# U's high part times both parts of x2 in one 480-column product, with an identity product to add the second half

## The reference, cut to what matters

```python
h = jnp.einsum('chkd,cd->chk', u, xt)          # rows of expert_u times x2
a = gt * jax.nn.gelu(h, approximate=False)
return jnp.einsum('chk,chkd->cd', a, vv)       # rows of expert_v
```

## Time and profile before

| | |
|---|---|
| median of 3 runs | 2293.77 us |
| the profiled execution | 2294.18 us, its span 2292.4 us |
| TensorE matmul busy, granted clock | 2269.2 us (99%), 0.998 |
| VectorE / ScalarE / POOL busy | 1716.0 / 1115.2 / 627.4 us |
| the chain that ended last, by line | line 812 30%, line 494 19%, line 847 17%, line 497 12%, line 853 9% |

### The profile page before, as it was taken

How to read it: one execution, slowest core, us unless ns; L and a number is a source line. 1 busy time by engine, 2 the same in 40 slices (tenths; PEclk the granted TensorE clock), 3 DMA queues, 4 the chain that set the end, 5 groups by cost and what they waited for, 6 DMA issues and landing times.

```text
span 2292.4 us, 45385 instructions
## 1 busy us (share of the span) xinstructions
PE 2269.2 (99%) x15683; PEld 2109.4 (92%) x15683; DVE 1716.0 (75%) x2311; ACT 1115.2 (49%) x1477; POOL 627.4 (27%) x442
## 2 busy tenths in 40 slices
PE   9999999999999999999999999999999999999997
PEld 8888899888898899999999999999999998998996
DVE  5544566655744577999999999998788887776767
ACT  4444555553343344555555455554554445444444
POOL 1000100000001026878756656557100000004000
PEclk9999999999999999999999999999999999999999
DMA  9888644566454656888878888888998997778874
GB/s 368 268 269 270 196 148 148 163 212 220 156 184 132 193 170 138 188 197 193 195 198 196 198 194 194 198 196 205 304 336 307 320 312 250 256 267 284 304 227 143
DMA packets 334138, 509.80 MB, mean 222 GB/s; under 512 B 68688, under 2 KB 216400, under 8 KB 326512
## 3 DMA queue, kind: packets, MB, share of 16 engines
q1 hardware_dynamic: 284832, 441.69, 62.6%
q0 software_dynamic: 48528, 66.36, 11.9%
q10 hardware_dynamic: 704, 0.75, 0.1%
HBM read 485.33 MB, written 21.23 MB: 221 GB/s over the span
## 4 chain that ended last, share of the span: by engine, by line
PE 95%; DVE 2%; DMA 2%; ACT 1%; issue 0%; POOL 0%; DVEq 0%; SPq 0%; ACTq 0%
PE ps L812 30%; PE ps L494 19%; PE ps L847 17%; PE ps L497 12%; PE ps L853 9%; PE ps L525 3%; DMA v_raw<-in_peer_v_dram 2%; PE ps L533 1%; PE ps L731 1%; PE ps L756 1%; PE ps L483 1%; PE ps L552 0%; ACT v_hi L1262 0%; DVE v_lo L1951 0%; PE ps L793 0%; PE ps L647 0%
## 5 line engine op out<-in xcount | busy, mean ns | idle before, releaser
L1535 DVE TENSOR_TENSOR split_ring<-weight_ring,split_ring 128x1024 fp32r<-128x1024 f32 x288 | 351.3, 1228 | 297.8 <-ACT split_ring L999 285.7
L1442 POOL DMA_INDIRECT gates_scratch<-sb_gains x256 | 492.4, 1924 | 244.3 <-ACT sb_gains L1175 128.0
L812 PE MATMUL ps<-parts,u_hi 128*128 128x240 f32 x4096 | 498.7, 274 | 0.0
L847 PE MATMUL ps<-e_pair,v_hi 128*128 128x480 f32 x2016 | 478.7, 378 | 2.1 <-ACT v_hi L1262 1.6
L812 PEld LDWEIGHTS ps<-parts,u_hi 128*128 128x128 f32 x4096 | 477.2, 190 | 0.0
L999 ACT ACTIVATE split_ring<-weight_ring 128x1024 fp32r<-128x1024 f32 x288 | 302.9, 1058 | 337.0 <-PE ps L494 212.3
L1951 DVE TENSOR_TENSOR v_lo<-v_raw,v_hi 128x1024 fp32r<-128x1024 f32 x252 | 308.3, 1224 | 169.7 <-ACT v_hi L1262 168.8
L1180 ACT ACTIVATE u_hi<-u_turned 128x1024 fp32r<-128x1024 f32 x256 | 272.0, 1062 | 329.2 <-DVE u_turned L1810 257.2
L1262 ACT ACTIVATE v_hi<-v_raw 128x1024 fp32r<-128x1024 f32 x252 | 267.3, 1061 | 329.8 <-PE ps L853 265.8
L847 PEld LDWEIGHTS ps<-e_pair,v_hi 128*128 128x128 f32 x2016 | 359.8, 188 | 46.1 <-ACT v_hi L1262 2.4
L1810 DVE STREAM_TRANSPOSE u_turned<-u_raw 128x1024 f32<-128x1024 f32 x256 | 315.7, 1234 | 16.9 <-PE ps L812 15.2
(11 more groups left out here) (263 smaller groups left out, 1670.3 us busy)
## 6 DMA issues: line engine op xcount, KB each, us to landing
u_raw<-in_peer_u_dram SPq DMA_DIRECT2D x1024, 128.0 KB
v_raw<-in_peer_v_dram SPq DMA_DIRECT2D x256, 512.0 KB
weight_ring<-in_w_in_dram SPq DMA_DIRECT2D x96, 512.0 KB, 5.9
weight_ring<-in_w_mkv_dram SPq DMA_DIRECT2D x64, 512.0 KB, 3.8
gates_scratch<-temps POOLq DMA_DIRECT2D x16, 1024.0 KB, 7.4
weight_ring<-in_w_o_dram SPq DMA_DIRECT2D x32, 512.0 KB, 4.6
weight_ring<-in_w_mq_dram SPq DMA_DIRECT2D x32, 512.0 KB, 4.8
weight_ring<-in_w_mo_dram SPq DMA_DIRECT2D x32, 512.0 KB, 3.8
```

The costliest lines, as they stand in the source:

```text
L812: m = nc.tensor.matmul(ps[:, b, 0:ET], u[:, k * P:(k + 1) * P], x2T[n][kk][:, 0:ET], start=not done and kk == 0 and n == 0, stop=done and ...
L847: return nc.tensor.matmul(ps[:, tile, 0:PAIR], v_hi[slot][:, tile * P:(tile + 1) * P], e_pair[e][:, b * PAIR:(b + 1) * PAIR], start=start, ...
L1442: pool.indirect_dma_start(gates_by_one, bass.IndirectOffsetOnAxis(ap=idx_all[:, j:j + 1], axis=0), gate_all[:, j:j + 1], None, compute_op= ...
L1535: nc.vector.tensor_tensor(w_lo[j % SPLIT], raw[j % RAW], w_hi[j % SPLIT].bitcast(F32), ALU.subtract).then_inc(lo_ready, 1)
```

## The change

- A view `x2_hi_lo` of x2's two parts as [high, rest], 4096 columns apart.
- `split_unit`: 8 products of 480 columns (U's high part times [high, rest], 240 each) in place of 16 of 240. The product with x2's rest now lands in columns 240 to 479 of the bank. The 8 products of U's rest stay.
- `copy_rest`: when a block's second unit is done, ScalarE copies columns 240 to 479 to SBUF, rounded (`x_rest`). In its order this stands between the two `unit_hi` that precede `take_hidden`.
- `add_rest`: TensorE multiplies `x_rest` by the identity onto columns 0 to 239 of the bank (240 columns), after the first unit of the next block; the last block's stands inside V's first eight products. It waits for `rest_copied` and releases the GELU (`hidden_ready`, in place of `u_used`).
- Before the stage, ScalarE copies the identity once (`ident_parts`).

```diff
+        x2_hi_lo = p1_to_3.rearrange("p (m n) -> p m n", m=2)
...
+            def add_rest(i, b):
+
+                pe.wait_ge(rest_copied, i + 1)
+                nc.tensor.matmul(ps[:, b, 0:ET], ident_parts[:, :], x_rest[:, :], start=False, stop=True,
+                                 skip_group_check=True).then_inc(hidden_ready, 1)
+
+            def split_unit(i, h, slot, b, rest_before=True):
 
                 pe.wait_ge(u_hi_ready, i * 2 + (h + 1))
-                half_sums(u_hi[slot], (0, 1), False)
+                for k in range(KB // 2):
+                    kk = h * (KB // 2) + k
+                    nc.tensor.matmul(ps[:, b, 0:2 * ET].rearrange("p (m t) -> p m t", m=2),
+                                     u_hi[slot][:, k * P:(k + 1) * P], x2_hi_lo[:, :, kk * T:kk * T + ET],
+                                     start=kk == 0, stop=False, skip_group_check=True)
                 pe.wait_ge(u_lo_ready, i * 2 + (h + 1))
-                half_sums(u_lo[slot], (0,), True).then_inc(u_used, 1)
+                for k in range(KB // 2):
+                    kk = h * (KB // 2) + k
+                    m = nc.tensor.matmul(ps[:, b, 0:ET], u_lo[slot][:, k * P:(k + 1) * P], x2T[0][kk][:, 0:ET],
+                                         start=False, stop=False, skip_group_check=True)
+                m.then_inc(u_used, 1)
+                if h == 0 and rest_before:
+                    add_rest(i - 1, (b - 1) % 3)
...
                 for tile in (2, 3, 4, 5, 6, 7, 0, 1):
+                    if tile == 5:
+                        add_rest(NKEY - 1, (NKEY - 1) % 3)
...
+            def copy_rest(i, b):
+
+                act.wait_ge(u_used, i * 2 + 2)
+                nc.scalar.activation(x_rest[:, :], ps[:, b, ET:2 * ET], ACT.Copy).then_inc(rest_copied, 1)
+
             def take_hidden(i, b):
 
-                act.wait_ge(u_used, i * 2 + 2)
+                act.wait_ge(hidden_ready, i + 1)
                 nc.scalar.activation(E[:, bass.ds(i * ET, ET)], ps[:, b, 0:ET], ACT.Gelu).then_inc(gelu_ready, 1)
 
+            nc.scalar.activation(ident_parts[:, :], ident[:, :], ACT.Copy)
...
                     for h in range(2):
                         unit_hi(m * PER + (3 + 2 * b + h), (2 * b + h) % US)
+                        if h == 0:
+                            copy_rest(m * (PER // 2) + b, b % 3)
                     take_hidden(m * (PER // 2) + b, b % 3)
...
             act.wait_ge(u_used, UNITS - 1)
             expert_parts(0, 0, 1)
+            copy_rest(NKEY - 1, (NKEY - 1) % 3)
             take_hidden(NKEY - 1, (NKEY - 1) % 3)
             v_part(1, 16, 1)
```

More of the change, by code:

```diff
@@ L105, in layer_program @@
         r0, r1, r2, r3, r4, r5, r6 = [at(f"region{n}", HOME[n], RC) for n in range(7)]
-        p1, p3 = [at(f"parts{n}", HOME[n], RC, F32R) for n in (1, 3)]
+        p1_to_3 = at("parts1_to_3", HOME[1], 2 * RC, F32R)[:, :]
+        p1, p3 = p1_to_3[:, 0:RC], p1_to_3[:, RC:2 * RC]
         p4_to_0 = at("parts4_to_0", HOME[4], HOME[0] + RC - HOME[4], F32R)[:, :]
@@ L176, in layer_program @@
         E = at("experts", 0, NKEY * ET)
+        x_rest = at("x_rest", TA + 5120, ET, F32R)
+        ident_parts = at("ident_parts", TA + TEMPS - P, P, F32R)
         HALF = D // 2
@@ L322, in layer_program @@
         gelu_ready = sem("gelu_ready")
+        rest_copied, hidden_ready = sem("rest_copied"), sem("hidden_ready")
         g_landed, e_scaled = [sem(f"g_landed{s}") for s in range(2)], sem("e_scaled")
@@ L804, in _ @@
                 slices("cols", range(10, 16), pair, x2T, 1, 1)
[L806 to L814, removed]
-                pe.wait_ge(u_hi_ready, i * 2 + (h + 1))
-                half_sums(u_hi[slot], (0, 1), False)
-                pe.wait_ge(u_lo_ready, i * 2 + (h + 1))
-                half_sums(u_lo[slot], (0,), True).then_inc(u_used, 1)
+            def add_rest(i, b):
[3 more added lines that the diff above has]
+            def split_unit(i, h, slot, b, rest_before=True):
+                pe.wait_ge(u_hi_ready, i * 2 + (h + 1))
+                for k in range(KB // 2):
[3 more added lines that the diff above has]
+                                     start=kk == 0, stop=False, skip_group_check=True)
+                pe.wait_ge(u_lo_ready, i * 2 + (h + 1))
+                for k in range(KB // 2):
[5 more added lines that the diff above has]
+                    add_rest(i - 1, (b - 1) % 3)
             def split_block(i, b):
@@ L829, in _ @@
                     pe.wait_ge(gelu_ready, 1)
-                    split_unit(0, 0, 0, 0)
+                    split_unit(0, 0, 0, 0, rest_before=False)
                     key_products(PQ0 + NP // 2 - 1, 1)
@@ L1246, in _ @@
                         unit_hi(n * 6 + (done + 3 + 2 * b + h), (2 * b + h) % US)
+                        if h == 0:
+                            copy_rest(n * 3 + (done // 2 + b), b)
                     take_hidden(n * 3 + (done // 2 + b), b)
             unit_hi(UNITS - 1, (UNITS - 1) % US)
+            copy_rest(NKEY - 2, (NKEY - 2) % 3)
             take_hidden(NKEY - 2, (NKEY - 2) % 3)
```

## The result

The changed kernel takes 2297.90 us (median of 22 runs, 2295.52 to 2300.82), the kernel before 2293.97 us beside it (22 runs). The ratio is 1.0015, 95% interval [1.0009, 1.0021]: 3.4 us slower, between 2.1 and 4.8. The forecast was 0.4 us less than before, within 0.2%. The size is within what I called no change, but the measurement is fine enough to see it, and the sign is the other one.

What follows compares the result with a forecast made beforehand. TensorE's stream was taken to bound the kernel, VectorE nearly as full. Merging -14.8, identity products +14.3 and the border +0.1 summed to -0.4 us: 2293.8 us against the profiled 2294.18, or 2293.4 against the median; range 2289 to 2302.

Steps and rivals of the forecast that it cites:

- what I called no change: Whole kernel: about 0.2% (4.6 us) is what a measurement can tell from no change; chance of landing within it 0.70.
- the price of the merged products: TensorE in U's stage: a 480-column product costs 216.1 ns against 223.33 for two of 240, saving 14.8 us.
- the first panels' slope: First panels, moving operand in two runs: 0.4345 ns per column between 256 and 512 columns, giving 216.1 ns for 480.
- break-even: U's stage: at 216.3 ns per merged product the saving would just pay for the added identity products.
- my own case: U's stage: merged product between 214.1 and 218.6 ns and no new waits; chance 0.71.
- the border: Passage from U's stage to V: V's high part slips by about 0.8 us, mostly regained from ScalarE's idle time; estimate 0.1 us.
- The third term: TensorE in U's stage: 128 added identity products of 240 columns at 111.67 ns each cost +14.3 us.
- no wait of TensorE in the stage: U's stage: no wait of TensorE for ScalarE or VectorE appears between 920 and 1600 us.
- ScalarE's copies hidden: ScalarE in U's stage: 128 copies of 0.39 us, 50 us on an engine about half busy, cost 0.
- VectorE as a floor: Search-loop pass of U's stage: VectorE's 47.88 us sets the pace if TensorE, at 48.24, gains over some 0.36 us.
- my list of signs: Signs expected in the profile after, among them 13763 products, a merged group at 1.73 us and a block of 5.35 against 5.36.
- The first rival: U's stage: merging saves little, a merged product costs 219 to 223 ns, total 2303 to 2308 us; chance 0.15.

Runs made afterwards that it cites:

- e3: Changed kernel with the merged products' moving operand as one run of 480 columns instead of two of 240; 2299.39 us, ratio 1.0023.
- e6: Changed kernel with one fixed moving operand for all merged products, one run of 480 columns from the start of x2's parts; 2301.69 us.
- e7: Changed kernel with one fixed moving operand for all merged products, one run beginning at column 480 of x2's parts; 2304.81 us.
- e8: Changed kernel with the moving operand's two runs of 240 columns beginning at multiples of 240 columns instead of 256; 2304.75 us.
- e9: Changed kernel with the merged products of a group going to three banks in turn; 2297.55 us.
- e10: Changed kernel with merged products going to three banks in turn and one fixed moving operand in one run; 2300.44 us.
- e13: Changed kernel with both runs of the merged products' moving operand begun 4 columns (16 bytes) later; 2296.04 us.
- e14: Changed kernel with both runs of the merged products' moving operand begun 8 columns (32 bytes) later; 2296.65 us.
- e15: Changed kernel with both runs of the merged products' moving operand begun 16 columns (64 bytes) later; 2295.24 us.
- e16: Changed kernel with the first slice of U's high part as stationary operand of all eight merged products of a group; 2297.69 us.
- e11: Kernel before with one wait added: the GELU of block 126 waits for the unit after the block; 2293.83 us, ratio 1.0002.
- e2: Changed kernel with merged products taken apart into 16 of 240 columns per unit; copy, identity product and waits stay; 2310.42 us, ratio 1.0070 to the kernel before.
- e1: Changed kernel without copy_rest and add_rest, GELU waiting for u_used again, second half never added; 2287.66 us, ratio 0.9972 to the kernel before.
- e5: Changed kernel with POOL adding the second half after ScalarE copies both halves out, no identity product; 2334.66 us, ratio 1.0178 to the kernel before.

## Why the prediction was wrong

The step that failed is the price of the merged products. I took 216.1 ns from the first panels' slope, with break-even at 216.3 and bounds of 213.8 and 223.3. In place it is 217.4 ns: a saving of 5.9 ns instead of 7.23, 12.1 us instead of 14.8. That alone turns -0.4 into +2.3. The measured price is inside my own case (214.1 to 218.6 ns), so the way of reasoning and the range held, and the size of this one term did not. Half of the groups in rows 3 showed nearly this price, 217.5 ns, and I had averaged it away. The form was the same as in the row I chose; the start of the moving operand and the columns were not, and e3, e6 to e10 and e13 to e16 show that the start and the number of runs move it by 3.5 ns. What makes just 217.4 ns of it here stays open. With a sum that cancels to 3%, a point taken from another stage could not carry a sign, and my case should not have centred on it.

Second, the border. I had looked at the last GELU only and found 2.08 us of idle time ahead of it. The GELU of block 126 was the one that mattered: it stood ahead of V's first high part and began to wait a unit longer. I put 0.1 us, the trace shows 0.76 us more gap, and e11 gets it from one wait. The step "where a wait is added, name what is queued behind it" was done for TensorE and for the loop, and left out here.

The third term held: 14.3 us for the identity products (e2: 111.67 ns each); beside merged ones they cost 114.1, together 14.6. The sum with the measured prices is -12.1 + 14.6 + 0.8 = +3.3 us, against a measured 3.4.

What held besides: no wait of TensorE in the stage, ScalarE's copies hidden, VectorE as a floor just below. It would have capped a better price, and in e1 it did, at 47.77 us for a pass where I had 47.9. (The block of 5.35 us in my list of signs was a slip: its own terms, 16 x 216.1 + 17 x 111.67 ns, make 5.36, no less than before.) The first rival (little saved) had the right direction, with 5.9 ns between its 2.5 and my 7.2, but not the size: it began at 219 ns. The rule of the Trainium skill, page "TensorE: Matmul & The Clock Gate", section "Back-to-back issue gap", which the page gives for a single matmul by itself and not for a stream, gave 2.5 ns saved and an estimate of +8.0 us. The trace agrees with its sign and not with its numbers: 217.4 ns for 480 columns and 111.67 for 240, where it makes 202.5 and 102.5.

No version here beats the kernel before with the whole sum computed. The 7.2 us that the merged products can free in e1 are less than the 14.3 us that TensorE needs to add the halves, and POOL's additions, as e5 places them, cost 41 us.

## What to carry to other kernels

Joining two products that share a stationary operand saved here only what an instruction costs beside its columns, 5.9 ns of 223; the product added to bring the halves together cost its full columns. Count both before anything else: one 240-column product costs as much as about 19 joined ones save, and here there were 16 for each. Where such terms nearly cancel, take a price from another stage as a range (here 213.8 to 217.5 ns in rows 3 alone) and say that the sign is open. When a result is made to come a step later, look at the last turn of the loop by itself, and at who stands behind it in the queue of the next stage.

## What the runs showed of the hardware

- The mean price of a 480-column product changes with where its moving operand begins and in how many runs: 216.6 to 220.1 ns in the same stream (e3, e6 to e10, e13 to e16). It also changes with the product's place in the block, from 212.5 to 224.1 ns with one and the same operand (e6). 240-column products by themselves take 111.67 ns on average (e2).
- With merged products the time of a block is a multiple of 6.67 ns in every variant: 5366.7, 5373.3, 5380, 5400, 5406.7, 5426.7, and a unit of e1 behind the search 2633.3. Without them it need not be: e2's 49 x 111.67 = 5471.7 is none, while the 5360 of the kernel before is one. A change of operand moves it in steps; what sets the step was not tried.
- A POOL addition of 240 columns took 1.78 us on average, and where it overlapped them some of VectorE's operations took longer: a subtraction of 1024 columns 1.48 us for 1.18, a comparison of 512 columns 1.18 for 0.67, a conversion of 32 columns with one input 0.67 for 0.17. The turning of 1024 columns and the search for the largest eight did not change (e5).
